# A MoE layer on one core: the first slot tile's products are regrouped, and warming matmuls are added between the counts and the gather

## What is computed

```python
def _moe(hn, w_group, b_group, w_router, b_router, w_up, w_down):
    t = hn.reshape(b * n, d)
    ...
    wv, idx = lax.top_k(pe, TOP_K)
    wv = wv / jnp.sum(wv, axis=-1, keepdims=True) * pg[:, None]
    ids = g[:, None] * EXPERTS_PER_GROUP + idx
    ...
    hid = jnp.einsum('td,edf->tef', t, w_up)
    a, u = jnp.split(hid, 2, axis=-1)
    act = jax.nn.silu(a) * u * gate.astype(hn.dtype)[..., None]
    y = jnp.einsum('tef,efd->td', act, w_down)
```

## Time and profile before

| | |
|---|---|
| device time, median of 3 runs | 830.07 us (828.58 to 830.39) |
| device time of the profiled execution | 828.55 us |
| its span, first to last instruction | 826.8 us |
| mean granted TensorE clock in it | 0.985 |
| PE busy | 786.3 us (95%) |
| DVE busy | 569.4 us (69%) |
| ACT busy | 368.7 us (45%) |
| POOL busy | 306.0 us (37%) |

### The profile page before, as it was taken

One profiled execution on the slowest core, in us unless ns is written; L12 is line 12 of the kernel. 1 busy time (PEld: TensorE's weight loads), 2 busy tenths in 40 slices (PEclk: granted clock), 3 DMA queues, 4 the chain that ended last, 5 costly groups with the idle time before them and its releaser, 6 DMA issues. The chain is left out here.

```text
span 826.8 us, 13559 instructions
## 1 busy us (share of the span) xinstructions
PE 786.3 (95%) x4858; PEld 619.4 (75%) x4859; DVE 569.4 (69%) x651; ACT 368.7 (45%) x680; POOL 306.0 (37%) x260
## 2 busy tenths in 40 slices
PE   7999999999989999998999999599999999999995
PEld 4879999999965566766667777388888888888641
DVE  5759966751047885875868767988567999573088
ACT  3661221221256963453536426645444444544254
POOL 2100799970010121100000010357466777564156
PEclk9999999999999999999999999799999999999997
DMA  9947645721056521320202238977878998889694
GB/s 314 377 143 252 204 147 159 224 58 46 1 187 232 162 81 52 103 77 27 77 26 77 66 114 291 329 251 236 302 266 330 414 392 275 297 305 369 207 367 191
DMA packets 78563, 165.86 MB, mean 201 GB/s; under 512 B 7429, under 2 KB 32565, under 8 KB 76466
## 3 DMA queue, kind: packets, MB, share of 16 engines
q1 hardware_dynamic: 69418, 132.14, 46.1%
q0 software_dynamic: 7904, 28.84, 9.7%
q10 hardware_dynamic: 1192, 4.21, 1.6%
HBM read 132.57 MB, written 32.60 MB: 200 GB/s over the span
## 5 line engine op out<-in xcount | busy, mean ns | idle before, releaser
L2457 PE MATMUL psum<-we_hi,x_parts 128*128 x384 | 138.2, 405 | 0.8 <-ACT x_parts L2215 0.8
L2001 DVE TENSOR_TENSOR we_lo<-we_raw,we_hi 128x2048 fp32r<-128x2048 f32 x48 | 118.1, 2464 | 1.5
L480 PE MATMUL psum<-hn_hi,w_hi 128*128 128x364 f32 (+1 forms) x384 | 92.3, 332 | 2.0 <-DVE hn_lo L738 1.1
L480 PE MATMUL psum<-hn_lo,w_hi 128*128 128x364 f32 (+1 forms) x384 | 91.4, 329 | 0.0
L480 PE MATMUL psum<-hn_hi,w_lo 128*128 128x364 f32 (+1 forms) x384 | 91.2, 328 | 0.0
L2000 DVE CAST we_hi<-we_raw 128x2048 fp32r<-128x2048 f32 x44 | 60.0, 1363 | 39.2 <-DMA we_raw<-in_w_up_dram 23.8
L2457 PEld LDWEIGHTS psum<-we_hi,x_parts 128*128 128x128 f32 x384 | 72.8, 190 | 15.4 <-issue 1.1
L1220 PE MATMUL psum<-wo_hi,mixin 128*128 128x512 f32 (+1 forms) x256 | 83.4, 397 | 0.6 <-DVE logits L1591 0.6
L2457 PE MATMUL psum<-we_lo,x_parts 128*128 x192 | 75.9, 395 | 0.0
L754 DVE SCALAR_TENSOR_TENSOR proj<-wm,cT,proj 128x2048 f32<-128x2048 f32 x28 | 72.8, 2648 | 2.5 <-DMA wm<-in_w_mod_dram 2.5
L480 PEld LDWEIGHTS psum<-hn_hi,w_hi 128*128 128x128 f32 x384 | 67.4, 189 | 5.2 <-issue 1.9
(11 more groups left out here) (383 smaller groups left out, 1592.3 us busy)
## 6 DMA issues: line engine op xcount, KB each, us to landing
we_raw<-in_w_up_dram SPq DMA_DIRECT2D x32, 1024.0 KB, 6.7
wm<-in_w_mod_dram SPq DMA_DIRECT2D x16, 1024.0 KB, 5.7
we_raw<-in_w_down_dram SPq DMA_DIRECT2D x16, 1024.0 KB
w_raw<-in_w_in_dram SPq DMA_DIRECT2D x16, 512.0 KB, 6.7
we_raw<-ff_d SPq DMA_DIRECT2D x12, 512.0 KB, 7.2
proj<-in_x_prompt_dram SPq DMA_DIRECT2D x4, 1024.0 KB, 8.5
sc_room<-in_w_mod_dram SPq DMA_DIRECT2D x4, 1024.0 KB, 11.4
wo_raw<-in_w_out_dram SPq DMA_DIRECT2D x2, 2048.0 KB, 11.3
```

Of the source, the lines that this page charges most:

```text
L480: mm = pe.matmul(psum[:, 2 * c + slot, 0:n], w[:, slot, k, :], hn[:, k, t0:t0 + n], start=(k == 0 and w is w_hi and hn is hn_hi), stop=(k ...
L2001: dve.tensor_tensor(we_lo[:, a:b], raw, we_hi[:, a:b].bitcast(F32), ALU.subtract).then_inc(ready, 1)
L2457: mm = pe.matmul(psum[:, bank, :], x[:, s, k, :], w[:, bass.ds(at + k * 2 * DE, 2 * DE)], start=(k == 0 and x is x_hi and w is we_hi), sto ...
```

## The change

Two edits, both in PE's program of `block_c`.

The first: 4 matmuls whose results nobody reads (`stay_warm(5, 4)`, into bank 5) are issued between the counting matmuls and `by_slot(6, ...)`, and those behind it are 5 now rather than 4.

The second: tile 0 has a function of its own, `up_first`. It issues for k = 0 to 3 the two products with `x_hi` (they wait for `xh_copied`, ACT's high copy, and no more for `x_ready`), then `lower_first(0)`, then the same for k = 4 to 7 and `lower_first(1)`, and last the eight products with `x_lo`, with `step0(k)` between these. Products and sums are the same 24 as before.

```diff
+            def stay_warm(bank, n):
+
+                for _ in range(n):
+                    pe.matmul(psum[:, bank, :], ident[:, :], ident[:, None, :].broadcast_to([P, 4, P]), start=True, stop=True)
+
+            stay_warm(5, 4)
             by_slot(6, ont_ids, 0, 1, True)
             pe.wait_ge(act_staged, V_STAGED + TILES)
-            for n in range(4):
-                pe.matmul(psum[:, 4, :], ident[:, :], ident[:, None, :].broadcast_to([P, 4, P]), start=True, stop=True)
+            stay_warm(4, 5)
             pe.wait_ge(tables_ready, 1)
...
             def up(t, s, place, copied, between, bank=2):
                 e, at = place
-                if not (isinstance(t, int) and t == 0):
-                    pe.wait_ge(x_ready, t + 2)
+                pe.wait_ge(x_ready, t + 2)
...
                 for k in range(KC):
-                    if isinstance(t, int) and t == 0 and k % (KC // 2) == 0:
-                        pe.wait_ge(x_ready, 1 + k // (KC // 2))
                     if k % (KC // 2) == 0:
...
+            def up_first(place):
+                e, at = place
+
+                def product(k, x, w):
+                    return pe.matmul(psum[:, FIRST_BANK, :], x[:, 0, k, :], w[:, bass.ds(at + k * 2 * DE, 2 * DE)],
+                                     start=(k == 0 and x is x_hi and w is we_hi), stop=(k == KC - 1 and x is x_lo))
+
+                for half in range(2):
+                    pe.wait_ge(xh_copied, 1 + half)
+                    pe.wait_ge(up_ready, e * 2 + (1 + half))
+                    for k in range(4 * half, 4 * half + 4):
+                        product(k, x_hi, we_hi)
+                        product(k, x_hi, we_lo)
+                    lower_first(half)
+                for k in range(KC):
+                    if k % 4 == 0:
+                        pe.wait_ge(x_ready, 1 + k // 4)
+                    mm = product(k, x_lo, we_hi)
+                    if k == KC - 1:
+                        mm.then_inc(up_done, 1)
+                    step0(k)
...
             turn_first(1)
-            lower_first(0)
-            lower_first(1)
-            up(0, 0, first, None, step0, FIRST_BANK)
+            up_first(first)
             pe.wait_ge(oneh_ready, 3)
```

## The result

The changed kernel takes 835.56 us (median of 6 runs, 831.9 to 836.4), the kernel before, run beside it, 829.54 us (6 runs, 828.38 to 831.35). The ratio is 1.0057, 95% interval 1.0037 to 1.0076. It is slower by 3.1 to 6.3 us, 4.7 us by the ratio (the two medians lie 6.0 apart). A later run of both on another occasion gave 1.0050 (1.0031 to 1.0068). The forecast said slower, with 831.8 us and a range up to 834.0, and the measured median lies above that range. The sign was right, and the loss about twice the +2.4 us of the sum.

What follows compares the result with a forecast made beforehand. PE was taken as the bound from tile 1 on, so a shift of tile 1's start shifts the end. -0.1 + 1.3 - 0.9 + 1.5 + 0.6 = +2.4 us on a mean of 829.4 gave 831.8 us, range 829.2 to 834.0.

Steps and rivals of the forecast that it cites:

- Four more warming matmuls: Behind the counts, beside DVE's table work: they cost nothing, and a faster `by_slot(6)` brings the gather forward, -0.1 us.
- Rival C: Ahead of `by_slot(6)`: the warming matmuls delay the gather by up to 2.3 us, giving 832.3 to 834.1 us; chance 0.14.
- The new wait for ACT: Ahead of tile 1's `lower_x`: PE idles some 3.6 us for ACT's high copy, queued behind two weight copies.
- Rival B: At `lower_x(1, 1)`: ACT's weight copies are out of its way, tile 1 starts 2.7 us earlier, 826.7 us; chance 0.10.
- What order alone costs, +0.4: At tile 1's start: `lower_x` comes 1.3 us later, fewer products behind it give back 0.9, together +0.4 us.
- DVE: DVE's third and fourth subtractions wait for ACT's weight copies and end at about 544, at no cost.
- The slow stretch behind the wait, +1.5: Behind PE's wait for tile 1's high copy: the clock falls to 1.2 GHz, +1.5 us within bounds of 0 and 1.84.
- The slow stretch at tile 0, +0.6: At tile 0's first products: the clock may fall around the transposes, +0.6 us within bounds of 0 and 1.6.
- The rule of the Trainium skill on transposes: At tile 0's transposes: transpose work does not count as TensorE busy, making the last term 1.6, the sum 3.4.
- Rival A: PE stays at 2.4 GHz through the new wait and tile 0: sum +0.3, 829.7 us, no change; chance 0.24.

Runs made afterwards that it cites:

- warm to the gather: The changed kernel with 7 rather than 5 warming matmuls behind `by_slot(6)`; median 833.66 us, ratio 1.0057 to the kernel before.
- busy in the wait: The changed kernel with 4 dummy matmuls issued ahead of tile 1's late `lower_x`; median 833.1 us, ratio 1.0037 to the kernel before.
- `lower_x` last: Changed kernel with weight copies ahead of tile 0's low copies, 7 warming matmuls, and tile 1's `lower_x` behind the last product; 829.63 us, ratio 0.9989.
- only the products: The changed kernel with the warming matmuls as before, so only the products are regrouped; median 835.17 us, ratio 1.0055 to the kernel before.

## Why the prediction was right in sign and wrong in size

By its own steps:

- *Four more warming matmuls.* Right. They took 3.7 us, ended a microsecond before `by_slot(6)`, and this ended 6.3 us after the counts began, as before. In four of the eleven profiles with these matmuls the clock fell during the counts, before them; they then took 5.0 to 5.2 us and `by_slot(6)` ended 0.1 to 0.2 us later. Rival C is real in kind and worth less than a tenth of its upper price of 2.3.
- *The new wait for ACT.* Right in its place, releaser and cause, with 3.0 us against "some 3.6". Moving the copies early confirms it. Rival B, in which these copies are out of the way, is what the version with the copies early and the clock held builds by hand: its 2.7 us were forecast, and 1.5 is what the distance shows.
- *What order alone costs, +0.4.* Too small by some 0.4. With both slow stretches taken off the changed kernel (18.1 - 2.8 - 1.7 = 13.6), 0.8 us remain. The full-clock pieces of two runs give the same: from tile 0's transposes to `lower_x` 544.73 - 533.35 = 11.4 us (warm to the gather), from there to tile 1 2.2 (busy in the wait). No run holds the clock at both places with ACT's queue as it is. I took the start of `lower_first` (532.78) as the moment at which a product could start, 1.2 us behind the transposes. The first product starts 1.8 to 2.0 us behind them in all profiles of the new order, 0.6 behind the end of the first high copy, the one it waits for (and 0.12 to 0.17 behind the end of the second), just as tile 0's first product before stood 0.6 behind the end of the first low copy. `lower_first`, whose address is fixed, started 0.05 behind its copy there. With `lower_x` last tile 1's first product, too, stands 0.64 behind its low copy, and there is only one copy there. Between wait and product stand the register instructions that make the weight address; that they are the reason was not tested.
- *DVE.* Right. Its third and fourth subtractions came later than forecast (542.64 to 547.13), still 2.2 us before `by_slot(7)` ended.
- *The slow stretch behind the wait, +1.5.* Right: 1.7.
- *The slow stretch at tile 0, +0.6.* **This is the step that failed.** It measured 2.8, outside even its bound of 1.6. Two things were wrong. With 0.6 of 1.6 I set the chance of the fall at less than one half, from the row in which 1.21 us of idleness ahead of the gather did no harm. With 2.0 to 2.6 us there, the clock fell at the transposes or at the first product in seven of seven profiles. With 0.4 to 1.2, in six, it held through the transposes. And I bounded the price by eight products. The stretch lasted from 532.1 to 538.9 in the profile, twice as long as that of before (535.1 to 538.5), although PE was busy in 5.9 of its 6.8 us, and covered 12 products and one `lower_first`. The bound of 1.6 holds where the stretch is short: with only the products it lasted 3.4 us, and the two groups took 5.5 us against 3.9 in the run that holds the clock. In the six profiles in which the clock fell earlier than that, by the transposes, the stretch lasted 6.8 us each time.

The forecast had 0.4 + 1.5 + 0.6 = 2.5 for the distance, and the terms measure 0.8 + 1.7 + 2.8 = 5.3. That the three add up to it follows from how the 0.8 was found; the check is the 13.6 from the pieces of the other runs. The measured loss by the ratios is 4.2 to 4.7.

In two of the seven profiles the clock fell just before the transposes started (by 0.15 and 0.03 us), in four during them and in one at the first product. In the first two, how transposes count cannot have decided the fall, and the others do not separate it from the gap. The rule of the Trainium skill on transposes (TensorE: Matmul & The Clock Gate, Part 4: PE-mode transpose), which would have made the last term 1.6 and the sum 3.4, was on the better side, but these profiles don't show it at work.

Rival A (the clock holds) is refuted for this kernel, whose clock fell at both places in both profiles, and the trace of the version with the copies early and seven matmuls shows what it would take.

## What to carry to other kernels

Before an engine's work is brought forward, follow the results that now come later on the engine that makes them: here PE's early products held back two ACT copies, and what stood behind these in ACT's program, 3.7 us of work for others, became PE's wait. Such work belongs in the gap that the new order opens, and not behind the next tile's copies either, where the loss comes back a tile later. Warming matmuls kept the clock here only where they reached up to the work that they were to warm and no two further gaps followed (the old order, 0.35 and 0.79 us, lost it all the same), and the medians show a gain from them only with the queue put right.

## What had not been expected

- The gap ahead of the gather splits the profiles cleanly: with up to 1.2 us (six profiles) the clock holds through the transposes, with the new order of products (four of them) through tile 0's sixteen high products as well; from 2.0 us on (seven) it has fallen by the first product. What lies between no run shows.
- A slow stretch can last long although TensorE is busy: 6.8 us at 1.2 GHz in the changed kernel, in which it worked for 5.9 us and stood idle for 0.9 near the start. Where the idleness lay ahead of the fall instead (only the products) the stretch was 3.4 us.
- Where the slow stretches fall differs between executions of one kernel: the tail has one in some profiles and none in others, and so have the stretches before the counts. Single runs of one kernel differ by 3 to 8 us (826.44 to 833.61 for the kernel before in one series of 35), as much as the whole effect of the change or more. The clock goes with it: these two executions have mean granted clocks of 0.988 and 0.981, and over the 35 time and clock have a correlation of -0.84.
